# First attention of a two-block kernel: scores two quads ahead, scaling and leasts in turn, other buffer counts

## What is computed

```python
s = q @ k.T * scale - slope * dist          # where valid, else -1e30
p = softmax(s)                              # the sliding window adds exp(sink) to the sum
o = p @ v                                   # times a gate for the three branches of the first eight heads
```

## Time and profile before

| | us |
|---|---|
| median of 3 runs | 1626.7 (1621.56 to 1628.99) |
| the profiled execution | 1627.72 |
| its span | 1626.4 |
| the first attention's quads in it | about 146 to 291 |

### The profile page before, as it was taken

How to read it: one execution, slowest core, us unless ns; L and a number is a source line. 1 busy time by engine, 2 the same in 40 slices (tenths; PEclk the granted TensorE clock), 3 DMA queues, 4 the chain that set the end, 5 groups by cost and what they waited for, 6 DMA issues and landing times.

```text
span 1626.4 us, 22505 instructions
## 1 busy us (share of the span) xinstructions
PE 1509.1 (93%) x8093; PEld 1291.7 (79%) x8093; DVE 1133.0 (70%) x2372; ACT 617.4 (38%) x1536; POOL 711.6 (44%) x668
## 2 busy tenths in 40 slices
PE   5998777999999999999999999999998999899997
PEld 4787445788878887887799899889986787899886
DVE  7646566467777669647867677777777588777764
ACT  3314566231212220113454554454455355344431
POOL 6756000347767748685444034303435114524430
PEclk8997799999999999999999999999998999999999
DMA  6623000424444436553321011101102321211221
GB/s 186 196 78 99 6 1 1 143 72 150 138 128 123 139 98 222 190 193 106 123 66 40 14 53 53 32 22 52 53 27 78 124 96 52 58 48 40 65 91 52
DMA packets 115887, 142.61 MB, mean 88 GB/s; under 512 B 11048, under 2 KB 75200, under 8 KB 115776
## 3 DMA queue, kind: packets, MB, share of 16 engines
q1 hardware_dynamic: 89968, 91.77, 18.5%
q10 hardware_dynamic: 25808, 49.40, 9.3%
HBM read 132.74 MB, written 8.40 MB: 87 GB/s over the span
## 4 chain that ended last, share of the span: by engine, by line
PE 66%; DVE 15%; ACT 7%; POOL 5%; issue 4%; DMA 1%; ACTq 0%; SPq 0%; DVEq 0%; POOLq 0%
PE ps L510 18%; PE ps L512 17%; PE ps L511 17%; POOL w_lo L499 3%; PE ps L1290 2%; POOL w_hi L497 2%; PE ps L1486 2%; PE ps L924 1%; PE ps L982 1%; DVE st L2911 1%; ACT p L2130 1%; DVE newton L2375 1%; PE ps L948 1%; DVE p L2579 1%; PE ps L1500 1%
## 5 line engine op out<-in xcount | busy, mean ns | idle before, releaser
L497 POOL TENSOR_SCALAR w_hi<-w_raw 128x512 fp32r<-128x512 f32 x308 | 236.6, 768 | 639.2 <-PE ps L512 481.1
L499 POOL TENSOR_TENSOR w_lo<-w_raw,w_hi 128x512 fp32r<-128x512 f32 x316 | 443.3, 1403 | 30.4 <-ACT w_hi L1676 4.7
L510 PE MATMUL ps<-w_hi,h_hi 128*128 128x384 f32 (+2 forms) x768 | 278.4, 363 | 8.2 <-POOL w_lo L499 2.9
L512 PE MATMUL ps<-w_hi,h_lo 128*128 128x384 f32 (+2 forms) x768 | 265.8, 346 | 0.0
L511 PE MATMUL ps<-w_lo,h_hi 128*128 128x384 f32 (+2 forms) x768 | 265.4, 346 | 0.0
L510 PE MATMUL ps<-h_hi,w_hi 128*128 128x512 f32 (+1 forms) x616 | 244.5, 397 | 6.4 <-DVE h_lo L2405 2.6
L512 PE MATMUL ps<-h_hi,w_lo 128*128 128x512 f32 (+1 forms) x616 | 237.1, 385 | 0.0
L511 PE MATMUL ps<-h_lo,w_hi 128*128 128x512 f32 (+1 forms) x616 | 237.0, 385 | 0.0
L2629 DVE SCALAR_TENSOR_TENSOR mod_acc<-mod_piece,csil,mod_acc 128x512 f32<-128x512 f32 x140 | 160.3, 1184 | 19.1 <-DMA mod_piece<-in_ada_w 15.1
L510 PEld LDWEIGHTS ps<-w_hi,h_hi 128*128 128x128 f32 x768 | 146.8, 191 | 20.7 <-POOL w_lo L499 4.3
L511 PEld LDWEIGHTS ps<-w_lo,h_hi 128*128 128x128 f32 x768 | 147.2, 192 | 8.6 <-issue 0.5
(11 more groups left out here) (337 smaller groups left out, 2990.3 us busy)
## 6 DMA issues: line engine op xcount, KB each, us to landing
mod_piece<-in_ada_w ACTq DMA_DIRECT2D x96, 256.0 KB, 3.2
w_raw<-in_w_gate_up SPq DMA_DIRECT2D x88, 256.0 KB, 3.2
w_raw<-in_a_w_in SPq DMA_DIRECT2D x128, 128.0 KB, 2.3
w_raw<-in_w_down SPq DMA_DIRECT2D x22, 512.0 KB, 4.4
w_raw<-in_b_w_in SPq DMA_DIRECT2D x20, 512.0 KB, 3.7
w_raw<-in_w_out SPq DMA_DIRECT2D x16, 512.0 KB, 3.8
w_raw<-in_w_in SPq DMA_DIRECT2D x8, 512.0 KB, 3.8
w_raw<-in_w_o SPq DMA_DIRECT2D x8, 512.0 KB, 3.8
```

The lines of the kernel that those rows point to most:

```text
L497: pool.tensor_scalar(hi[:, e, :], raw[:, e, :], 1.0, 0.0, ALU.mult, ALU.add).then_inc(*s["pool_step"].up())
L499: m = pool.tensor_tensor(lo[:, e, :], raw[:, e, :], hi[:, e, :], ALU.subtract)
L510: pe.matmul(out, a[0], b[0], start=start, stop=False)
L512: return pe.matmul(out, a[1], b[0], start=False, stop=stop)
```

## The change

- `SLOTS_P` goes from 8 to 12 and `SLOTS_T` from 12 to 8; together they use the same memory.
- `slots_behind`: before the first quad the slots of the first two quads (0 and 1) are done, and beside quad n those of quad n+2. For tiles 2 and 3, kinds 0 and 1, that is eight slots ahead where it was four.
- `VALUES_AT_ONCE` goes from 2 to 1: a part of values is done as soon as it is due.
- `dve_quad_scale` becomes a generator that stops after each head. VectorE now does beside quad n: the reciprocal and first head of quad n+1, then a slot's leasts of quad n+2 and one head more of quad n+1, in turn, then what is left of the scaling.

```diff
-SLOTS_P = 8
-SLOTS_T, SLOTS_T_EARLY = 12, 5
+SLOTS_P = 12
+SLOTS_T, SLOTS_T_EARLY = 8, 5
@@ def slots_behind(qs, n):
-    total = qs[-1].slots[-1] + 1
-    return range(0, 4) if n < 0 else [i + 4 for i in qs[n].slots if i + 4 < total]
+    if n < 0:
+        return range(0, qs[1].slots[-1] + 1)
+    return qs[n + 2].slots if n + 2 < len(qs) else range(0)
@@
-VALUES_AT_ONCE = 2
+VALUES_AT_ONCE = 1
@@ def dve_quad_scale(k, dve, qs, q):
-    m.then_inc(*s["b_scaled"].up(q.n))
+        if e == PER_G - 1:
+            m.then_inc(*s["b_scaled"].up(q.n))
+        yield
@@ def dve_quads(k, dve):
-    dve_quad_scale(k, dve, qs, qs[0])
+    for _ in dve_quad_scale(k, dve, qs, qs[0]):
+        pass
@@
     for q in qs:
+        scaled = dve_quad_scale(k, dve, qs, qs[q.n + 1]) if q.n + 1 < len(qs) else iter(())
+        next(scaled, None)
         for slot in slots_behind(qs, q.n):
             dve_slot_least(k, dve, qs, slot)
-        if q.n + 1 < len(qs):
-            dve_quad_scale(k, dve, qs, qs[q.n + 1])
+            next(scaled, None)
+        for _ in scaled:
+            pass
```

## The result

The changed kernel takes 1617.2 us (median of 19 runs, 1612.9 to 1625.9) beside 1626.7 (19 runs, 1621.6 to 1634.2) before. The ratio of runs taken side by side is 0.995, with a 95% interval of 0.9937 to 0.9964: about 8 us faster, between 6 and 10 (the two medians by themselves are 9.5 us apart). Forecast were 19.5 us and a time of 1608; 1617.2 lies inside the range of 1598 to 1619, near its upper end.

What follows compares the result with a forecast made beforehand. A ring of dependences among TensorE, VectorE and ScalarE in the first attention, not one engine's limit. Gains of 7 + 3.5 + 5 + 4 = 19.5 us from 1627.7 give 1608.2, said as 1608; range 1598 to 1619.

Steps and rivals of the forecast that it cites:

- ring through the scaling: First attention: turns, scores, leasts, exponentials and scaling wait on each other in one row, 6.9 us a quad.
- Tile 0: First query tile of the first attention: start 3.4 us sooner, length 26.1 to some 25.5 us, gain 4 us.
- Tile 1: Second query tile, 256 wide: from 32.9 to 28 us if the clock is full, gain 5 us.
- Tile 2: Third query tile, 384 wide: from 36.6 to 33 us, gain 3.5 us.
- Tile 3: Fourth query tile, 512 wide: from 42.2 to 35 us, gain 7 us.
- Fewer holes should mean fewer such falls: TensorE's clock in the first attention: fewer idle gaps, fewer drops to 0.50; tile at 0.83 could come near 1.
- copies' ring: ScalarE's queue in the first attention: copies stand behind exponentials and delay a quad's second turn, about 5.5 us a round.
- A: Rival: ScalarE's order and the four banks keep rounds near their present length; gain 8 to 12 us, 1617; chance 15%.
- B: Rival: clock stays at 1.2 GHz through the second query tile and more of the third; gain 10, 1617; chance 10%.
- Rival C: Rival: values one at a time wait on TensorE for copies behind exponentials; slower, 1638; chance 6%.
- D: Rival: the banks bind, so scores two quads ahead don't arrive; no change, 1627; chance 4%.
- E: Rival: clock full from the first query tile on, rings reach engine sums; gain 28 to 35 us, 1596; chance 8%.

Runs made afterwards that it cites:

- e6: The kernel before, with values one at a time and one slot of exponentials behind each copy on ScalarE: 1636.6 us, ratio 1.0064 to the kernel before.
- e7: The changed kernel with next-slot scores repeated on TensorE before five turns that had waited for copies: 1612.0 us, ratio 0.9916 to the kernel before.
- e8: The changed kernel, but ScalarE does all copies of a quad first, then all exponentials: 1611.4 us, ratio 0.9909 to the kernel before.
- e12: e3 with next-slot scores repeated on TensorE before turns 12 and 18: 1610.3 us, ratio 0.9891 to the kernel before.
- e3: The changed kernel, but ScalarE puts one slot of exponentials behind each copy instead of two behind every second: 1611.4 us, ratio 0.9889 to the kernel before.
- e4: The kernel before with one edit of the change alone, values one part at a time: 1622.5 us, ratio 0.9967 to the kernel before.
- e1: The changed kernel, but VectorE does all leasts of quad n+2 before scaling quad n+1: 1621.6 us, ratio 0.9957 to the kernel before.
- e11: The kernel before with next-slot scores repeated on TensorE before eight turns, two to five times each: 1623.7 us, ratio 0.9972 to the kernel before.
- e2: The changed kernel, but VectorE scales all of quad n+1 before the leasts of quad n+2: 1620.2 us, ratio 0.9954 to the kernel before.
- e9: e8 with next-slot scores repeated on TensorE before turns 1, 4, 5 and 6 in the first query tile: 1615.1 us, ratio 0.9921 to the kernel before.

## Why the prediction failed

The bound was read rightly: the stage alone changed, what follows took 1336.1 us for 1335.8, and a gain in the stage was carried whole. The ring through the scaling was read rightly too: TensorE's waits for scalings went from 24.9 to 9.9 us (under 8 were foretold), and e6 shows that the exponentials had to leave that ring first. The sum of 19.5 us was wrong. By its terms, against the stage's 5.4 us:

- Tile 0, forecast 4: the start came 3.4 us sooner, as reckoned, but the length grew from 26.1 to 28.1, gain 1.4. TensorE's own work, forecast at 24.7 us, measured 22.8 (three of the four parts of values fall into the tile); the length of 25.5 made of it left no room for the 5.3 us in which TensorE is idle there. VectorE is busy 19.6 us where it was 15.9, since leasts of tile 1 now fall into tile 0. The working counted TensorE's share of that and not VectorE's.
- Tile 1, forecast 5 "if the clock is full": it was 0.89, gain 0.9. At 1.00 it takes 28.8, 27.8 and 28.5 us (e7, e8, e12), and 28 was forecast.
- Tile 2, forecast 3.5: gain 0.3. The clock fell to 0.86. At 1.00: 31.7, 31.8 and 30.9, forecast 33.
- Tile 3, forecast 7: gain 2.9 at 0.91. At 1.00: 36.6 (e7) and, with one slot between the copies, 33.9 (e12); forecast 35. From first turn to first turn its four wide quads take 9.6, 9.9, 6.4 and 7.7 us and the two narrow ones 5.8; forecast were 6.2, 7.8, 5.5, 5.5 and 5.5, and before they took 9.5, 9.8, 8.0, 9.2 and 5.8. In e12, with the full clock and shorter waits for copies, they take 7.9, 8.6, 5.4, 6.3 and 5.8.

So the tiles' lengths, with what had been added for handing over and shortfall, were about right for a full clock and for copies that hardly wait. The step that failed is the sentence on the clock, "Fewer holes should mean fewer such falls". TensorE's idle time in tiles 1 to 3 went from 24.9 to 17.3 us and the falls from six to four, but the time at the low clock did not shrink (some 22 us before, some 24 after): the change lengthened the holes on the copies before turns 12, 26 and 44 (1.74 to 2.64 us, 0.79 to 1.84, 1.33 to 2.40) and left 1.78 us on a copy before turn 54, where a scaling had kept TensorE for 4.21. These four were each followed by a fall. e7 takes the falls of tiles 1 to 3 away and leaves the order of the useful work as it is: by the profiles that is 10.8 us of the 14.1 missing there (19.5 - 5.4), by the ratios 5.5 of the 11.4 missing (19.5 - 8.1), about half in the typical run. The second failing step is the copies' ring. It was named ("stands behind exponentials") and priced at 5.5 us a round, where the third and fourth quad of tile 3 took 6.4 and 7.7, and at nothing in the first two, which were priced by the engines' own sums of 6.2 and 7.8 us and took 9.6 and 9.9. The price was without the output that stands in the same queue and with the leasts at the old pace in part; in the first quad of tile 3 the hole was 2.4 us and the next one 1.2. The two together are nearly all of it: e3, which moves one exponential out from before each copy, gives 0.61% more than the changed kernel, 9.9 us (between 6 and 14) of the 11.4, part of it wait and part clock; its ratio is a gain of 18.1 us. e8 and e12 have stages of 126.6 and 125.4 us, where the forecast had put it at 125.1.

Rivals A and B, 15% and 10%, each foretold 1617 by one of these two; they happened together, the first setting off the second. B came in part only: tile 1 was at 0.89 and not at the low clock throughout. That both give the measured 1617 is luck in the number, since neither was priced as it came. I had them as alternatives and priced the fall by the tile's work alone. The Trainium skill (TensorE: Matmul & The Clock Gate, "HAM oscillation — how this bites in real kernels") describes a matrix product in which TensorE waits for data in every round and then starts the next round at the half clock, so that each wait is paid for again in slower work. The traces agree in kind: a hole of 2.64 us in tile 1 was followed by about 7 us at 0.50.

Rival C, the values one at a time as a loss, is refuted by e4: they gain 0.33% on the kernel before. That term, 2 us of cost inside the shortfall, had the wrong sign. The values' waits for copies, to be over 10 us if C were right, are 0.5 us in all, where C needed 31 waits of 0.65. Rivals D (no change) and E (1596) didn't come. Of the signs named, the reciprocals' waits (16.5 to under 4) came out at 12.9: the exponentials are issued a round earlier, but in ScalarE's queue they stand behind copies, and these may wait for their turns. At the end of tile 1 the copy at 203.63 had waited 1.72 us for its turn, the exponentials behind it ended at 206.47, and the reciprocal at 206.51 had waited 1.16 us for them. e1 brings them to 0.6 and gains nothing by it, so they were covered. VectorE and ScalarE over 75% busy in tiles 2 and 3 was wrong (66% and 57%, 68% and 63%). A clock under 0.8 in tile 1 didn't come, but 0.86 in tile 2 did.

Open: how the change's 8 us divide between values one at a time and two quads ahead. e4's interval reaches from 0.9954 to 0.9980, and e7 against e11 says 9 us for all parts together at a full clock. The change minus its values can't be run, since the eight turned tiles need them: by the order of the programs copy 52 would wait for a value that stands behind turn 55 on TensorE, and turn 54 for copy 52.

## What to carry to other kernels

When a pipeline is made deeper, walk through each engine's queue and ask what small piece, for which the busiest engine waits, now stands behind large ones; here moving one exponential out from between copies doubled the gain. In a stage where TensorE has holes, look at the granted clock behind each long one before pricing any edit, since the work behind it may cost double (here it did behind four holes of 1.8 to 2.6 us, but not behind every hole of that length); an edit that takes waits away in sum but makes single ones longer can lose by that what it gains. A test that fills such holes with repeated work tells how much of the time is the clock's; its size is to be read from many runs, since single executions of the changed kernel lie up to 13 us apart.

## What the runs showed of the hardware

More work made the kernel faster: about 6 us of repeated passes took 10.8 us off the stage of the profiled executions and 0.34% off the kernel, by keeping the clock at 1.00 in tiles 1 to 3.

The clock of the changed kernel fell after holes on TensorE of 2.64, 1.84, 2.40 and 1.78 us (in front of turns at 184.97, 214.98, 252.62 and 270.75 us), and came back 4 to 10 us later. The length of a hole doesn't decide it. The first of these holes, and one in front of the turn at 200.63 after which the clock stayed up, with its window:

```profile
184.97 0.63 PE L925 MATMUL ps<-ident,p 128*128 128x128 f32 x4 [2.64 <-ACT pt_early L1769]
...
200.63 0.66 PE L925 MATMUL ps<-ident,p 128*128 128x128 f32 x4 [1.97 <-DVE p L2578]
```

```profile
200.00:202.50 2.50, 1.87 (x12) 1.24 (x12) 1.90 (x9) 1.59 (x6) 0.00 (x0) 1.00 0.00 0
```

The clock also stayed at 1.00 behind holes of 2.12 us in e8 (turn at 220.43), 2.30 us in e1 (206.92) and 2.51 us in e6 (274.46), while it fell behind one of 1.60 us in e3 (185.19). The same hole, 1.97 us in front of turn 18, that went without a fall in the changed kernel had one in e3, beginning within the hole, before the turn's start at 201.46. What distinguishes these cases, no run here tells.

Tile 0 begins with a fall as well. The clock is at 1.00 until just before the first score, in front of which TensorE waits for VectorE's queries:

```profile
144.98 0.44 PE L903 MATMUL ps<-k_hi_twice,q_stacked 128*128 128x128 f32 x1 [2.54 <-DVE q_stacked L2488]
```

```profile
144.00:144.50 0.50, 0.00 (x0) 0.00 (x0) 0.47 (x1) 0.49 (x3) 0.50 (x1) 1.00 0.00 0
...
145.00:145.50 0.50, 0.50 (x3) 0.50 (x3) 0.47 (x2) 0.00 (x0) 0.50 (x2) 0.50 0.00 0
```

This hole of 2.5 us stands in every kernel here, and the clock comes down to 0.50 between half a microsecond before and one and a half behind the first score in each. It came up again some 22 us after the first score in e2, e4 and e6, 24 in e11, 28 in e8, 30 in the changed kernel and 31 in e9, which had TensorE busy for 28.5 of 29.8 us. In e4, e6 and e11 it fell once more within the tile, behind a hole of 2.1 us. More busy time there did not go with an earlier rise.
